# RWKV chunk inverse: the level-masked blocks built by VectorE instead of GpSimd

## The reference, cut to what matters

```python
def _rwkv7_step(S, inp):
    r, w, k, v, a, b = inp
    sa = jnp.einsum('bhvk,bhk->bhv', S, a)
    S = S * w[:, :, None, :] + sa[..., None] * b[:, :, None, :] + v[..., None] * k[:, :, None, :]
    y = jnp.einsum('bhvk,bhk->bhv', S, r)
    return S, y
# ... y over all 512 tokens, 16 heads, then group norm, bonus, gate and a 1024x1024 product
```

## Time and profile before

| | |
|---|---|
| median of three timed runs | 2247.7 us (2247.57 to 2249.05) |
| profiled execution, its own time | 2245.14 us |
| its span, first to last instruction | 2243.3 us |
| TensorE busy | 2155.3 us, 96% |
| VectorE busy | 1305.1 us, 58% |
| ScalarE busy | 918.2 us, 41% |
| GpSimd busy | 115.7 us in 136 instructions |
| granted TensorE clock, mean | 0.987 of full speed |

### The profile page before, as it was taken

How to read it: one execution, slowest core, us unless ns; L and a number is a source line. 1 busy time by engine, 2 the same in 40 slices (tenths; PEclk the granted TensorE clock), 3 DMA queues, 4 the chain that set the end, 5 groups by cost and what they waited for, 6 DMA issues and landing times.

```text
span 2243.3 us, 38228 instructions
## 1 busy us (share of the span) xinstructions
PE 2155.3 (96%) x15190; PEld 1734.2 (77%) x15190; DVE 1305.1 (58%) x2047; ACT 918.2 (41%) x1533; POOL 115.7 (5%) x136
## 2 busy tenths in 40 slices
PE   6999999988999999989999999999999999999998
PEld 4866666676788888867788888888867887888887
DVE  5856767765654535776637636456755555434345
ACT  5854433434432323456655423234344444313222
POOL 0002212211000000100010000001000000000001
PEclk9999999989999999999999999999999999999999
DMA  4310000013232232211221333323211232333322
GB/s 141 96 44 15 16 29 16 25 40 132 76 103 93 94 99 81 73 44 31 68 76 48 105 101 94 102 83 96 71 47 43 85 108 91 96 96 101 95 87 71
DMA packets 54331, 169.02 MB, mean 75 GB/s; under 512 B 7064, under 2 KB 13464, under 8 KB 54064
## 3 DMA queue, kind: packets, MB, share of 16 engines
q1 hardware_dynamic: 54192, 167.07, 23.9%
HBM read 164.95 MB, written 2.10 MB: 74 GB/s over the span
## 4 chain that ended last, share of the span: by engine, by line
PE 86%; DVE 8%; ACT 3%; issue 2%; DMA 0%; SPq 0%; DVEq 0%; ACTq 0%
PE bank L2124 53%; PE bank L2718 3%; PE bank L2312 2%; PE bank L2277 2%; PE bank L2598 2%; PE bank L2209 2%; PE bank L2329 2%; PE bank L2159 2%; PE bank L2399 1%; PE bank L2411 1%; PE bank L2226 1%; PE bank L2635 1%; PE bank L2617 1%; PE bank L2243 1%; PE bank L2728 1%
## 5 line engine op out<-in xcount | busy, mean ns | idle before, releaser
L1279 DVE TENSOR_TENSOR w_lo<-w_raw,w_hi 128x1024 fp32r<-128x1024 f32 (+4 forms) x313 | 356.7, 1141 | 191.8 <-ACT w_hi L690 186.9
L2124 PE MATMUL bank<-a_hi,w_hi 128*128 128x512 f32 x1154 | 451.5, 391 | 2.1 <-DVE w_lo L1279 2.1
L2124 PE MATMUL bank<-a_lo,w_hi 128*128 128x512 f32 x1154 | 449.1, 389 | 0.0
L2124 PE MATMUL bank<-a_hi,w_lo 128*128 128x512 f32 x1154 | 449.1, 389 | 0.0
L690 ACT ACTIVATE w_hi<-w_raw 128x1024 fp32r<-128x1024 f32 (+4 forms) x313 | 301.4, 967 | 209.9 <-PE bank L2124 196.8
L2124 PEld LDWEIGHTS bank<-a_hi,w_hi 128*128 128x128 f32 x1154 | 216.6, 188 | 49.2 <-DVE w_lo L1279 2.5
L2124 PEld LDWEIGHTS bank<-a_hi,w_lo 128*128 128x128 f32 x1154 | 216.7, 188 | 45.9 <-issue 1.2
L2124 PEld LDWEIGHTS bank<-a_lo,w_hi 128*128 128x128 f32 x1154 | 216.6, 188 | 45.1
L2124 PE MATMUL bank<-b_hi,w_hi 128*128 128x512 f32 x520 | 202.9, 390 | 4.0 <-DVE down_kv L1840 3.4
L2124 PE MATMUL bank<-b_hi,w_lo 128*128 128x512 f32 x520 | 202.3, 389 | 0.0
L2124 PE MATMUL bank<-b_lo,w_hi 128*128 128x512 f32 x520 | 202.3, 389 | 0.0
(11 more groups left out here) (388 smaller groups left out, 3917.4 us busy)
## 6 DMA issues: line engine op xcount, KB each, us to landing
w_raw<-in_f0gu SPq DMA_DIRECT2D x44, 512.0 KB, 3.6
w_raw<-in_f1gu SPq DMA_DIRECT2D x44, 512.0 KB, 3.5
w_raw<-in_f2gu SPq DMA_DIRECT2D x44, 512.0 KB, 3.5
w_raw<-in_f0dn SPq DMA_DIRECT2D x16, 512.0 KB, 3.5
w_raw<-in_f1dn SPq DMA_DIRECT2D x16, 512.0 KB, 3.5
w_raw<-in_f2dn SPq DMA_DIRECT2D x16, 512.0 KB, 3.5
w_raw<-in_kl SPq DMA_DIRECT2D x12, 512.0 KB, 3.5
w_raw<-in_in SPq DMA_DIRECT2D x10, 512.0 KB, 3.5
```

The costliest lines, as they stand in the source:

```text
L1279: dve.tensor_tensor(lo[:, 0:n, :], raw[r][:, 0:n, :], hi[:, 0:n, :].bitcast(F32), ALU.subtract).then_inc(w_split[r], 1)
L2124: mm = pe.matmul(bank[r][:, :], w[r][:, k, :], a[:, k, :], start=(k == 0 and n == 0), stop=(k == kt - 1 and n == 2))
```

## The change

The ten masked blocks of a tile leave GpSimd's queue and enter VectorE's, with the same operands and mask. That of level 1 follows the transpose of the same p in `masks`; that of level lv+1 stands ahead of the add of level lv for the same p. GpSimd keeps k_dec and r_dec.

```diff
         @block.gpsimd
             for j in range(DT):
-                for lv in range(1, LEVELS + 1):
-                    for p in range(2):
-                        if lv == 1:
-                            pool.wait_ge(masked, j * 8 + (SCORES.index((p, 0)) + 1))
-                        else:
-                            pool.wait_ge(z_done, j * 2 * LEVELS + 2 * (lv - 2) + p + 1)
-                        mask = const("level", lo=lv * HEAD, hi=(lv + 1) * HEAD).unsqueeze(1).broadcast_to([P, TT, HEAD])
-                        pool.tensor_tensor(off[p][:, :, :], ab[p][:, :, :], mask, ALU.mult).then_inc(off_ready, 1)
-
                 if j + 1 < DT:
...
                         dve.transpose(flat(inv[p]), flat(inv_t[p])).then_inc(inv_ready, 1)
+                        off_blocks(q, 1, p)
+
+            def off_blocks(j, lv, p):
+                if lv > 1:
+                    dve.wait_ge(z_done, j * 2 * LEVELS + 2 * (lv - 2) + p + 1)
+                else:
+                    dve.wait_ge(masked, j * 8 + (SCORES.index((p, 0)) + 1))
+                dve.tensor_tensor(off[p][:, :, :], ab[p][:, :, :], each("level", lv * HEAD, (lv + 1) * HEAD), ALU.mult)\
+                    .then_inc(off_ready, 1)
...
                     for p in range(2):
                         b = 4 - 4 * p
+                        if lv < LEVELS:
+                            off_blocks(j, lv + 1, p)
                         dve.wait_ge(grown, j * 2 * LEVELS + (2 * (lv - 1) + p + 1))
```

## The result

| | before | changed |
|---|---|---|
| median | 2248.38 us (2247.57 to 2249.35, 4 runs) | 2261.69 us (2259.6 to 2262.48, 4 runs) |
| profiled execution: own time, span | 2245.14, 2243.3 us | 2259.6, 2257.8 us |
| granted clock, mean | 0.987 | 0.982 |

The ratio of changed to before is 1.0057, with a 95% interval of 1.0045 to 1.0069: 13.3 us slower, where 6.5 over these 2248.4 were forecast (7.2 over the median shown then) and the range ended at 2258.5.

The account below looks back on a forecast made before the run. VectorE was taken as the engine TensorE waits for where the change adds work. Six steady tiles 5.9, first tile 0.9, last 0.4: 7.2 us over the 2247.7 median gave 2254.9 us, range 2246.5 to 2258.5.

Parts of the forecast that it names:

- Price c = 0.33 us: Start-to-start time that one 128x256 masked block adds to a VectorE queue that never idles: 0.33 us.
- Step 4: Steady tile, level 4: two blocks in VectorE's unbroken queue, less a 0.20 us wait; the add shifts +0.65 us.
- The bounds of c: A block's price between 0.24 and 0.41 us; steady tile 0.62 to 1.30 us, sum 4.7 to 9.9 us.
- Given back: Seed's predicated copies, no longer contended by GpSimd's blocks: 0.47 us back on each slow copy, -0.14 at level 1's growth product.
- The sign named for it: Level 1: the profile after would show TensorE's wait for ak, 0.29 us before, shorter.
- Steps 1, 2, 3, 5: Steady tile: level 1 -0.14 us, level 2 nothing, level 4 start +0.19, second z of level 5 +0.98.
- GpSimd's lateness (the faster rival): TensorE's loads released by GpSimd were real stops, 6.8 us in all, so the change is faster: 2240.9 us; 6%.
- the held block: Level 5: a block on VectorE waits for GpSimd's running k_dec, some 0.9 us a tile: 2261 us; 5%.
- The clock: Level 5's longer gap drops TensorE from 2.4 to 1.2 GHz: 2260 us for one tile, 2285 for six; 5%.
- the half case: Levels 4 and 5: only part of the delay counts, some 0.5 us a steady tile: 2251.4 us; 16%.
- no change: Levels 3 to 5 hide their blocks in gaps, only -0.14 us a tile remains: 2246.8 us; 12%.
- Tile 7: Last tile, VectorE full: four blocks in the queue, about 1.25 us, less returned time: +0.4 us, between 0 and 1.2.

Follow-up runs that it names:

- filled pair: Changed kernel and kernel before, each with one unused matmul in TensorE's gap at level 5, tiles 0 to 6: 2257.8 and 2250.0 us.
- mended pair: VectorE's y_n, k_fac and k_new moved behind the adds and transposes: 2253.2 us with all blocks on VectorE, 2246.1 with all on GpSimd.
- first set of runs: The changed kernel as first timed, 2261.7 us; the second set is the same kernel timed once more, 2259.2 us.
- mended order: VectorE's y_n moved behind level 2's p=1 add and transpose, k_fac and k_new behind level 4's; 2250.1 us with six blocks on VectorE, four on GpSimd.
- lv5_pool: Changed kernel with only the two blocks of level 5 given back to GpSimd: 2253.7 us.
- reorder_after: Changed kernel, all blocks on VectorE, with y_n, k_fac and k_new moved behind the adds and transposes that z waits for: 2253.2 us.
- lv5_dve: Kernel before with only the two blocks of level 5 moved to VectorE, levels 1 to 4 on GpSimd: 2258.1 us.
- fill_else: Changed kernel with the same unused matmul in tiles 0 to 6, but ahead of level 2, where TensorE has no gap: 2263.4 us.
- fill_before: Kernel before with one unused matmul on TensorE between the two z of level 5, tiles 0 to 6: 2250.0 us.
- fill_after: Changed kernel with one unused matmul on TensorE between the two z of level 5, tiles 0 to 6: 2257.8 us.

## Why the prediction was wrong

- **Direction and mechanism: right.** VectorE's queue is the path in levels 3 to 5, and the blocks lengthen it.
- **Price c = 0.33 us: right to 0.05.** The add starts 0.31 us (322.14 to 322.45) and 0.33 us (324.29 to 324.62) after the block in front of it, and 0.28 behind the reciprocals. Step 4 had +0.65 where +0.54 came: the block behind the scan moved the add by only 0.02 us (1.37 us from scan to add before, 1.39 now), not by c - 0.20 = 0.13.
- **The bounds of c: a slip.** A steady tile is 5c - 0.67 (the 0.34 of "4c - 0.34" holds one block more, at c = 0.33), so c = 0.24 gives 0.53 us and c = 0.41 gives 1.38, not 0.62 and 1.30. The forecast itself is not touched.
- **Given back: right.** All copies at 0.45 us; -0.15 at the growth product. The sign named for it was wrong: TensorE's wait for ak grew from 0.29 to 0.41 us, since its z no longer waits and it arrives earlier.
- **Steps 1, 2, 3, 5: right** to 0.1 us a tile. Five of the six tiles, those without a fall, grew by 0.73 to 1.10 us, where 0.98 was forecast. Tile 0 cost 0.78 us up to its second z of level 5, where 0.9 was forecast. The sum of 7.2 us agrees with the filled pair, 7.8. The 7.1 of the mended pair lies as near, but by luck in part, since its blocks are paid at another place.
- **GpSimd's lateness (the faster rival), and the held block: neither came.** The kernel is slower, not faster. The block starts at 324.29, k_dec behind it at 324.51, and the longest of all 80 blocks took 0.427 us, so none waited for k_dec.
- **The clock: this is the step that failed.** The sum kept TensorE's clock at 1.00 in the steady tiles and left the fall as a rival of 5%, with the right mechanism and place (the gap of level 5). The runs showed falls to 0.50 behind that gap in one or two of six tiles, 3.1 and 3.3 us in the two profiles. The term that was missing is 13.0 less 7.8, some 5 us, by the first set of runs and 2 us by the second. That the rival's 2260 for one tile lies near the 2261.7 is luck: a tile in which the clock fell was 1.6 to 3.1 us longer in these profiles, not 5. The rows in hand said more than 5%: in tile 7 of the kernel before the clock fell behind waits of TensorE for a transpose of the same kind. The longest of them, 1.34 us (row below), is nearly the 1.5 us that the prediction itself gave the steady tiles. That the half case and no change held 0.28 together while this held 0.05 was the misjudgement, and it cut the range at 2258.5.
- **Tile 7: +0.4 forecast, nothing measurable** (2261.2 with its blocks given back).

The row of the kernel before, in tile 7, on which the judgement of the clock rests:

```profile
470.99 0.77 PE L2399 MATMUL bank<-rw_inv,rw_off 64*64 64x64 f32 x16 [1.34 <-DVE rw_inv L1665]
```

What is shown: the queue cost of a steady tile, step by step; and that with the gap filled the profiles have no falls in the steady tiles. That took 5.5 us (4.7 of them in the six tiles) off the kernel with level 5 on VectorE, and 3.9 or 1.4 us off the changed one. What is argued only: that the whole rest in the changed kernel is the clock. Its two profiles show 3.1 and 3.3 us of falls in the six tiles; the others lie behind 450 us, where the kernels without the change have falls too in every profile, and no run separates them there.

## What to carry to other kernels

An operation moved off a slow engine costs its full start-to-start distance on the faster one if it lands in an unbroken queue that another engine waits for; ask for each instance which wait ends last behind it, since in this order of the queue six of the ten were free and four made the loss. In the mended order the same six were not free (2250.1 against 2246.1), so the question has to be asked again for each order. Where TensorE's wait grows from 0.7 to over 1 us within a dense stretch, price the granted clock as a term and not as an accident, and test it with a filler in the gap. The fastest of all was the kernel before with k_fac, k_new and y_n moved behind the transposes that z waits for, by 2.3 us, barely clear of noise.

## What the runs showed of the hardware

- Waits of TensorE of 0.67 us (before), 0.90 us (lv5_pool) and 0.94 us (reorder_after) in each steady tile came with no fall in these tiles. With 1.02 us (lv5_dve) the clock fell in four of six tiles, and with 1.35 us (all blocks) in one or two, in one profile (fill_else) in none. The length of the single wait alone does not decide it. A fall went to 0.50 and lasted some 3 to 7 us.
- That VectorE and GpSimd exclude each other shows for the predicated copy, a tensor_scalar, a scan and scalar_tensor_tensor alike (0.45 and 0.92; 0.54 and 0.86; 1.16 and 1.42; 0.74 and 1.75 us). The one that started second was the longer, at distances of 0.03 us (295.64 and 295.67) to 0.56 us (320.28 and 320.84).
- All four kernels with a filler show stalls of TensorE with no releaser at the same line, of 0.65 us in the fourth tile of fill_before (43.38 us) to 1.03 us in the sixth of fill_after (44.65 us); without a filler no profile has one there. The first of fill_after:

```profile
330.47 0.33 PE L2482 MATMUL bank<-rw_rk,rw_v_nat 64*64 64x64 f32 x2 [1.00 <-issue]
```

Their cause is not known.
